# A decoder layer with 32 experts: gate and up weights with four neighbouring rows in each partition

## The reference

```
def expert(args):
    xb, e = args                                # xb: a block of tokens x 1024
    gu = (xb @ w_gu[e] + b_gu[e]).astype(f32)   # w_gu[e]: 1024 x 2048
    gate, up = jnp.split(gu, 2, axis=-1)
    ...
    return act.astype(x.dtype) @ w_down[e] + b_down[e]   # w_down[e]: 1024 x 1024
```

## Time and profile before

| | us |
|---|---|
| median of 3 runs (1522.27 to 1524.48) | 1523.48 |
| the profiled execution, its own time | 1523.85 |
| its span in the profile | 1522.1 |
| TensorE matmuls busy | 1460.3 (96%) |
| PE waits for expert pieces (L2388 and L2375), in all | 29.0 |

### The profile page before, as it was taken

One profiled execution on the slowest core, in us unless ns is written; L12 is line 12 of the kernel. 1 busy time (PEld: TensorE's weight loads), 2 busy tenths in 40 slices (PEclk: granted clock), 3 DMA queues, 4 the chain that ended last, 5 costly groups with the idle time before them and its releaser, 6 DMA issues.

```text
span 1522.1 us, 23099 instructions
## 1 busy us (share of the span) xinstructions
PE 1460.3 (96%) x9252; PEld 743.2 (49%) x9253; DVE 519.5 (34%) x980; ACT 263.2 (17%) x604; POOL 114.0 (7%) x100
## 2 busy tenths in 40 slices
PE   9999999999999998999999999999999999999896
PEld 7777776556777764333333333333333333333332
DVE  3652788767510146122122212211212112122123
ACT  1224214631210014100101101011001001100102
POOL 1002141010502402000000000000000000000000
PEclk9999999999999999999999999999999999999999
DMA  6346686556269647999999999999999999999995
GB/s 211 111 166 176 206 269 232 177 175 193 80 217 333 252 168 310 428 428 427 428 427 429 428 428 429 428 429 428 428 429 428 429 428 428 429 428 429 428 428 217
DMA packets 110285, 507.80 MB, mean 334 GB/s; under 512 B 12552, under 2 KB 49008, under 8 KB 85552
## 3 DMA queue, kind: packets, MB, share of 16 engines
q1 hardware_dynamic: 103548, 499.37, 81.9%
q10 hardware_dynamic: 6676, 7.56, 1.6%
HBM read 491.18 MB, written 15.72 MB: 333 GB/s over the span
## 4 chain that ended last, share of the span: by engine, by line
PE 61%; DMA 25%; DVE 3%; ACT 1%; issue 1%; DVEq 0%; SPq 0%; ACTq 0%
DMA wGU<-in_w_gu 23%; PE ps L2388 12%; PE ps L2393 11%; PE ps L1892 10%; PE ps L2375 5%; PE ps L2196 3%; PE ps L1906 3%; PE ps L2210 2%; PE ps L2302 2%; PE ps L2223 2%; PE ps L2336 2%; PE ps L2310 1%; DMA ringS<-in_ssd_proj 1%; ACT xs L1261 1%; PE ps L2323 1%
## 5 line engine op out<-in xcount | busy, mean ns | idle before, releaser
L2388 PE MATMUL ps<-wGU,xe 128*64 128x512 f32 x1536 | 342.2, 594 | 17.8 <-DMA wGU<-in_w_gu 17.1
L2393 PE MATMUL ps<-wD,aT 128*64 128x512 f32 x1024 | 226.8, 595 | 0.0
L2388 PEld LDWEIGHTS ps<-wGU,xe 128*64 128x64 f32 x1536 | 107.9, 137 | 233.4 <-issue 198.1
L1892 PE MATMUL ps<-xT,ring 128*128 128x288 f32 (+1 forms) x864 | 179.8, 409 | 1.2 <-PEq L200 0.7
L1892 PEld LDWEIGHTS ps<-xT,ring 128*128 128x128 f32 (+1 forms) x864 | 125.1, 170 | 46.0 <-issue 3.5
L2393 PEld LDWEIGHTS ps<-wD,aT 128*64 128x64 f32 x1024 | 70.7, 137 | 131.8 <-issue 127.9
L2375 PE MATMUL ps<-wGU,xe 128*64 128x512 f32 x512 | 121.3, 594 | 11.9 <-DMA wGU<-in_w_gu 11.9
L1785 DVE TENSOR_SCALAR sg<-sg 128x512 f32<-128x512 f32 x32 | 13.7, 427 | 334.3 <-ACT sg L1256 334.3
L1792 DVE COPY ysb<-ps 64x512 f32<-64x512 f32 x32 | 22.2, 694 | 304.8 <-PE ps L2397 304.8
L1256 ACT ACTIVATE sg<-ps 128x512 f32<-128x512 f32 x32 | 19.1, 597 | 470.2 <-PE ps L2380 470.2
L396 PE MATMUL ps<-xT,ring 128*128 128x288 f32 x320 | 78.1, 407 | 0.0
(11 more groups left out here) (476 smaller groups left out, 1442.6 us busy)
## 6 DMA issues: line engine op xcount, KB each, us to landing
wGU<-in_w_gu SPq DMA_DIRECT2D x128, 2048.0 KB, 37.0
wD<-in_w_down SPq DMA_DIRECT2D x64, 2048.0 KB, 37.0
ring<-in_w_in SPq DMA_DIRECT2D x21, 2048.0 KB, 9.3
out<-hst SPq DMA_DIRECT2D x8, 1024.0 KB, 5.8
ringS<-in_ssd_proj SPq DMA_DIRECT2D x4, 2048.0 KB, 11.1
wbuf<-prompt_A_rows ACTq DMA_DIRECT2D x16, 384.0 KB, 3.9
out<-Sb SPq DMA_DIRECT2D x2, 2048.0 KB
ring<-in_hg_proj SPq DMA_DIRECT2D x2, 2048.0 KB, 8.6
```

The lines of the kernel that those rows point to most:

```text
L1892: last = m.matmul(ps[h, b, 0:T], ring[c % 2][:, k, n * P + h.start:n * P + h.stop], xT[:, k, :], start=(k == 0), stop=(k == KD - 1))
L2388: last = m.matmul(ps[half[h], bank, :], xe[:, f, hx, :], wgu[n][:, k, col + CW * h:col + CW * h + CW], start=(i == 0 and k == 0), stop=False)
L2393: last = m.matmul(ps[half[h], B_Y, :], aT[:, k, i - 4, :], wdn[n][:, k, CW * h:CW * h + CW], start=(i == 4 and k == 0), stop=False)
```

## The change

Gate and up pieces are laid out in twos. A pair of pieces covers 512 rows of `w_gu`, of which partition p gets rows 4p to 4p+3. Piece 2m holds rows 4p and 4p+1 of its 512, piece 2m+1 holds rows 4p+2 and 4p+3. So a piece is still 16 KB for each of 128 partitions, but the runs in memory stand 32 KB apart, and the other piece has what lies between. `turn_x` picks columns with a step of four to match. `w_down` pieces stay as they were.

For expert 0's pieces ahead of the blocks there is a new function, `piece_pair`: it loads both buffers of a pair with two DMAs, the first for partitions 0 to 63 and the second for partitions 64 to 127, each with one 32 KB run a partition (2 MB each). The second semaphore of the pair is waited for together with the first in block 0 (`paired`).

```
-        wgu = [at(f"wGU{i}", kb, [P, 2, 2 * D]) for i, kb in enumerate(buf_kb)]
+        wpair = [at(f"wGU{i}", buf_kb[2 * i], [P, 4, 2 * D]) for i in range(5)]
+        wgu = [wpair[i // 2][:, 2 * (i % 2):2 * (i % 2) + 2, :] for i in range(10)]
...
-                    src, dst, r = (w_gu, wgu[n], 256 * i) if i < 4 else (w_down, wdn[n], 512 * (i - 4))
-                    rows = 256 if i < 4 else 512
-                    sp.dma_start(dst[:], src[0, bass.ds(e, 1), r:r + rows, :].rearrange("a (p k) n -> p (a k) n", p=P)).then_inc(sem, 16)
+                    src, r, j = (w_gu, 512 * (i // 2), i % 2) if i < 4 else (w_down, 512 * (i - 4), 0)
+                    k = 2 if i < 4 else 4
+                    dst = wgu[n] if i < 4 else wdn[n]
+                    rows = src[0, bass.ds(e, 1), r:r + 512, :].rearrange("a (p k) n -> p (a k) n", p=P)
+                    sp.dma_start(dst[:, :, :], rows[:, k * j:k * j + k, :]).then_inc(sem, 16)
+
+                def piece_pair(i):
+
+                    rows = w_gu[0, 0, 256 * i:256 * i + 512, :].rearrange("(p k) n -> p k n", p=P)
+                    for h in range(2):
+                        sp.dma_start(wpair[i // 2][64 * h:64 * h + 64], rows[64 * h:64 * h + 64]).then_inc(m_w[i + h], 16)
...
-                for i in range(2):
-                    piece(0, i, i, m_w[i])
+                piece_pair(0)
...
-                for i in range(2, 4):
-                    piece(0, i, i, m_w[i])
+                piece_pair(2)
...
-                    src = xs[:].rearrange("q (i p k) -> q i k p", i=2, k=2)
+                    src = xs[:].rearrange("q (p k) -> q k p", k=4)
                     for f in range(4):
-                        last = m.transpose(ps[:, B_XT, f * P:(f + 1) * P], src[:, f // 2, f % 2, :], ident[:])
+                        last = m.transpose(ps[:, B_XT, f * P:(f + 1) * P], src[:, f, :], ident[:])
...
                         pe.wait_ge(m_w[n], loaded)
+                        if paired and i in (0, 2):
+                            pe.wait_ge(m_w[n + 1], loaded)
```

More of the change, by code:

```diff
@@ L2343, in scatter, with run @@
                         (prompt(j, B_S + j % 3) if j < 4 else samples(B_S + j % 3)).then_inc(m_s, 1)
-                def run(b, turn0, first, pair, places=None):
+                def run(b, turn0, first, pair, places=None, paired=False):
                     pe.wait_ge(m_xc, b + 1)
@@ L2409, in _ @@
                 pe.wait_ge(m_ok, 1)
-                run(0, 0, 0, None)
+                run(0, 0, 0, None, paired=True)
                 run(1, 0, 6, None, (6, 7, 8, 9, 0, 1))
```

## The result

The changed kernel takes 1543.18 us (median; 1542.26 to 1543.44), against 1522.88 for the kernel before (its three runs of the table above and one more). The ratio is 1.0118 with a 95% interval of 1.0096 to 1.0139: 20.3 us slower. The forecast was 1539.4, with a range from 1530 to 1548. The profiled execution took 1543.2 us, 19.35 more than the profiled one of before, and its span is 1541.5 us against 1522.1. The two differences are not the same because the profiled execution of before was 0.97 us above that median and this one 0.02.

A forecast was written before the change was run, and what follows sets the result against it. TensorE's chain sets the pace to 560 us, full DMA engines at 428 GB/s from about 600 us. Terms 9.8 + 1.6 + 3.7 + 0.8 = 15.9 us gave 1539.4 us against the median, range 1530.0 to 1548.0.

The forecast's parts named there:

- the half rate: First expert's pair loads: a transfer to 64 partitions moves at half of 428 GB/s, so a pair takes 19.6 us.
- the two waits: TensorE waits about 10.7 us for `ringS` near 500 us and 3 to 4 us for `w_out` near 560.
- the narrow bands: Bias tables loaded into 32-partition bands at 476 to 480 us: 196 and 205 GB/s with engines fully busy.
- first pair, resumption of L2196: Ahead of the blocks, pieces 0 and 1 delay `ssd_proj`'s last quarter, which has no slack: +9.8 us.
- low clock behind it: After each stall TensorE's clock drops to 0.50: +1.6 us after the first, +0.8 us after the second.
- wait for `w_out`: Pieces 2 and 3 take 9.8 us more against 6.1 us slack before `w_out`'s first half: +3.7 us.
- rest up to block 0: Between the second stall and block 0: no further term; the load stream starts as much later as TensorE.
- the blocks and the end: From block 0 on: the full load stream cannot catch up, so the delay reaches the end one for one.
- The loop: Expert blocks: runs 32 KB apart and `turn_x`'s step of four cost 0; loads stay at 428 GB/s.
- the halves run at full rate: Rival for the first expert's pairs: they take 9.8 us as now, total 1523.5 us; chance 0.09.
- the spacing slows the loop: Rival: wider-spaced runs slow the blocks' loads, up to 28.0 us on top of the forecast, 1567.4; chance 0.06.
- faster: Rival: engines exceed 428 GB/s and halves cost nothing; at most all piece waits vanish, 1494.5 us; chance 0.05.

## Why the prediction was right, and where its sizes were off

The mechanism held at every step: the half rate, the two waits and where they stand, and a loop without change. The sizes came out at the top of what I had allowed: the bounds of the sum were 12.6 and 20.1 us, and 19.4 (the profiled executions) and 20.3 (the medians) were measured. The views that gave it were the half rate of the narrow bands, the landing of `ssd_proj` 0.02 us before TensorE went on the earlier trace rows, and the slack of 6.1 us before `w_out`. The terms, from the same places of the two timelines:

| step | predicted | measured | from |
|---|---|---|---|
| first pair, resumption of L2196 | +9.8 | +10.75 | 500.26 to 511.01 |
| low clock behind it | +1.6 | +2.96 | 15.79 to 18.75 us for 64 matmuls |
| wait for `w_out` | +3.7 | +3.70 | none to 3.70 |
| low clock behind it | +0.8 | +1.52 | 1.95 to 3.47 us |
| rest up to block 0 | 0 | +1.0 | 19.94 at block 0, less the four above |
| the blocks and the end | 0 | -0.6 | 19.4 at the end of the span |
| sum | 15.9 | 19.3 | |

**The pair.** I took half of 428 GB/s; the half rate is 201 to 207, what the bands' row had said (205). With 205 the pair takes 20.5 us, or 10.7 more, which was my upper bound and what came out. The wait on the page grew by more, from 0.93 to 12.95 us, but TensorE had come 1.27 us earlier to this point in this execution (498.06 against 499.33). Such a lead is lost in the wait and is no part of the change. Where a stall absorbs it, the point of resumption is to be compared, not the wait.

**The clock.** This is the term that was too small. The clock stayed at 0.50 not for 3.1 us after dense work had begun again, as in the earlier trace rows, but from 511.01 to about 517.0 (0.74 in 516:518), 6.0 us; 6.0/2 = 3.0 us lost by that, 2.96 by the matmuls' own times. I had 3.2 as the upper bound and should have chosen nearer to it: one example in one trace is a weak centre. Nor does this loss go with the length of the stall: 2.96 us were lost behind 12.95 us of waiting, 2.4 behind 11.65, 2.9 behind 4.86 and 2.6 behind 3.62 (the second stall of the run with two queues). The stall of 3.7 us brought the clock down as well (window 564:566 of the changed kernel has 0.71), which I had given one half.

**The rest up to block 0.** The first matmul of L2288 (L2295 in the changed kernel) has moved by 18.99 us, from 591.36 to 610.35, which is the four steps above to within 0.1. The other 0.95 us arise between it and block 0. In both kernels the clock falls once more in this thin stretch of the router: it is down from about 587.6 to 594.5 before and from about 609.2 to 616.0 now. The stretches are equally long, but counted from that matmul the second lies 2.6 us later, so more of it falls on busy matmuls. The other traces go with this: where the drop lies 0.5 us later than before (only the first pair by halves), 0.2 us are added, and where it lies 0.2 us earlier (the pair behind `ssd_proj`), 0.1 us is gained. The layout alone, which has neither of the two long stalls, has it 2.9 us later and adds 1.1 us. So this term varies from trace to trace, and it comes without the halves too. That the place of the drop makes all of it is read from these traces and not tested.

**The loop** went as forecast: the layout and the step of four are free (ratio 0.9999). The weight loads of `turn_x` take 211 ns, 2 more than before, as `turn_a`'s did.

Of the rivals, "the halves run at full rate" fell with the profile, "the spacing slows the loop" with the run of the layout alone, and "faster" with 428 GB/s in the loop and with the 32 KB runs over all partitions, which gained nothing.

No version beats the kernel before beyond the measurement: whole pieces in either layout, even and odd partitions, or one transfer a pair are all within 0.1% of it.

## What to carry to other kernels

A load queue that is written in one order is as critical as its tightest follower: before a transfer is reshaped, look at what lands behind it and how many microseconds later it is needed. Keep transfers over the whole range of partitions; if they must be split, split them by even and odd, not into the lower and upper half. Between long runs the distance in memory is free here, and what counts is the size of a packet. When a stall is priced, allow one to three microseconds for TensorE's clock behind it, even if the stall is short.

## What the runs showed of the hardware

- Transfers to partitions 0 to 63 or 64 to 127 move 201 to 207 GB/s with all engines busy, with runs of 16 or 32 KB. When the two halves came from two queues, one was moved after the other, at 207 GB/s. Transfers to every other partition move 432. A packet of 32 KB takes 2.56 us in the first case and 1.21 us in the second.
- Packets of 8 KB instead of 16 for the gate and up pieces lower a full stream from 428 to 423 or 424 GB/s, whether the runs stand 16 KB or 1 MB apart. The time grew by 9.0 and 9.1 us. By the rates the stream of 890.7 us becomes up to 1.2% longer, 10.5 us. 120 pieces with 8 more packets on each of 16 engines are 960 more an engine, so a packet costs about 9 to 11 ns (an estimate from these numbers). Packets of 32 KB, in the one pair where they were tried, gained nothing that could be seen.
- In eight stalls of TensorE of 3.6 to 13.0 us, in five runs, the granted clock fell to 0.50 (1.2 GHz). After the stall of 12.95 us it stayed there for 6.0 us of dense work, after one of 3.70 us for about 3.2. The matmuls behind a stall took 1.3 to 3.1 us longer in all, and this did not grow with the stall: 1.3 to 2.6 us after three stalls of 3.6 to 3.8 us, 2.9 after one of 4.9, and 2.4 to 3.1 after four of 10.5 to 13.0.
